# Latent attention's queries and keys as high and low parts, its logits in three fp32r passes in place of one fp32 product

## The chip, the cores and the metric

The kernel runs as one program on one NeuronCore of one Trainium2 chip. The metric is the device time of an execution in microseconds (us), the median of three runs. The profile is of one execution, taken by the hardware profiler; its times count from the start of the span. PE is the matrix engine (TensorE), ACT the ScalarE, DVE the VectorE, POOL the GpSimd, SP the engine that issues the loads.

## The reference

Two layers of a first kind (gated spatial mixing, a state-space mixer, differential attention, a feed-forward network) are followed by two layers of a second kind, over 512 positions and a width of 1024, in float32. The change lies in the second kind, in the logits of its latent attention:

```python
q = (rms_norm(q_lat, q_a_norm) @ w_qb).reshape(b, s, 8, 96)
kv = (rms_norm(kv_lat, kv_a_norm) @ w_kvb).reshape(b, s, 8, 64 + 64)
...
q, k = rms_norm(q, q_norm), rms_norm(k, k_norm)      # then rope on the last 32 of 96
sc = jnp.einsum('bqhd,bkhd->bhqk', qb, k) * 96 ** -0.5
sc = jnp.where(causal, sc, NEG_INF)
p = jax.nn.softmax(sc, axis=-1)
o = jnp.einsum('bhqk,bkhd->bqhd', p, v)
```

Beside it a layer has a short gated convolution and a sliding-window attention, each with a silu gate, and one output projection with a residual.

## The kernel before

Every large product is made of three passes of type fp32r: an operand x is kept as a high part (x rounded to fp32r) and a low part (x minus the high part), and `mm3` adds high x high, high x low and low x high in PSUM. Weights come by DMA in slabs of up to 1024 columns into a ring of four (`w_raw`); ACT writes the high part of a slab (`split_hi`, L564), DVE its low part over the raw one (`split_lo`, L569), three slabs ahead of PE (`hi_ahead`, `lo_ahead`).

The latent attention runs in sixteen steps of the loop `for g in range(FILLS)`, called fills here. Each engine has this loop in its own program, in a fixed order, and semaphores tie them together. Eight heads (h) times four blocks of 128 queries (qi) make 32 steps n = 4h + qi; fill g has steps 2g and 2g+1, so an even fill has the blocks with 128 and 256 keys of a head and an odd one those with 384 and 512. In a fill:

- PE multiplies one weight slab for the convolution or a gate (`slab_t`, eight groups k of three passes, L574 to L576). In an even fill it transposes, before group 5, the queries and the keys of head g/2 (`heads_t`, L674, four 128x96 transposes each) into two banks of PSUM. After the slab it waits until both banks have been read (`pm_left`), makes the logits of steps 2g and 2g+1 (L2439), and transposes the weights of the two steps before (`weights_t`, L674). Before group 6 of fills 5, 9 and 13 it multiplies the weights of two heads by V (`by_v`, L2413).
- ACT copies queries and keys of the head from PSUM to SBUF, times the norm's gain (`heads_in`, L1226), at the start of an even fill; copies transposed weights (`weights_in`, L1246) and takes the exponentials of the logits (`exponentials`, L1235); then splits a slab (`hi_ahead`).
- DVE takes the maximum of each row (`maximum`, L1865 to L1867), divides the exponentials by their sum (`weights`, L1873 and L1874), splits a slab (`lo_ahead`, L569), and does the convolution (L1842 to L1858) and the norm of the window attention (L1824 to L1833) in shares. `gated` (L1880), at the start of fills 5 and 9, multiplies the product with V by its gate and so frees its bank.

`qkt`, the queries and keys, has two buffers (h % 2). The four banks `pm` of PSUM are used in turn, in one fixed order for all engines: whoever wants the i-th use waits for the reader of use i - 4 (`take_pm`). So the banks of a head's transposes are those of the logits of the odd fill before, which the exponentials free; and the bank of a product with V is the one that the second transposes of weights in the same fill want.

Of the kernel before, what the change touches and what calls it, by code (L numbers as in the profile page):

```python
# [7 lines left out]
F32 = mybir.dt.float32  # L8
# [5 lines left out]
P = 128  # L14
# [99 lines left out]
def program(nc, t, out, depth=DEPTH, depth2=DEPTH):  # L114
    with ExitStack() as ctx:
# [62 lines left out]
        def at(off, n, shape=None, **kw):  # L178
            a = arena[:, off:off + n]
            return a.rearrange(shape, **kw) if shape else a  # L180
# [220 lines left out]
        sq2 = at(19456, 3072)  # L401
        mla_sq = [sq2, at(11264, 2048)]
        st2 = rinv[:, :]
        qkt = at(19456, 2048, "p (b c s) -> p b c s", b=2, c=2)

        PT_AT = [sum(SEQ - P * j for j in range(kt)) for kt in range(TT + 1)]
        pt = at(11264, 2 * PT_AT[TT], "p (b n) -> p b n", b=2)
# [84 lines left out]
        def gate_unit(i):  # L492
# [15 lines left out]
                "ffn_hi_done": KD, "ffn_split": KD, "f_tap": 2 * FT, "f_step": 4 * FT, "f_silu": FT, "f_val": FT, "f_hi_done": FT, "f_split": FT}  # L508
        PER2 = {"par_landed": 16 * 13, "h_val": KD, "h_hi_done": KD, "h_lo_dve": len(LO_DVE), "h_lo_pool": len(LO_POOL), "lat_rms": 1, "lat_ready": 2 * TT,
                "lat_hi_done": 3, "lat_split": 3, "k_rot": 6, "mla_sq": 2, "mla_ssq": 2, "mla_rms": 2, "mla_rot": 1, "swa_sq": 2, "swa_ssq": 2,  # L510
                "swa_rms": 1, "swa_kd": TT, "cv_free": 4, "neg_max": MLA_H * TT, "w_ready": MLA_H * TT, "y_hi_done": 12, "y_split": 12,
                "swa_gates": 2, "mla_gate": 1, "rope_tab": 8, "s_max": SWA_H, "s_exp": SWA_H, "s_w_ready": SWA_H * TT, "alibi_landed": 16}

        def steps_of(h):
# [26 lines left out]
        def pmb(i):  # L541
            return pm[:, i % 4, :]
# [118 lines left out]
        def pm_filled(eng, i):  # L661

            eng.wait_ge(pm_ready, i + 1)
            return pmb(i)
# [177 lines left out]
        def _(act):  # L842
            chain = Chain(act, "act_step")

            def hi_ahead(s, m=0, it=0):

                if s + LEAD < len(WORDS):
                    split_hi(act, s + LEAD, m, it, WORDS[s + LEAD + (m * it if isinstance(it, int) else 0)])
# [288 lines left out]
            for l in range(depth2):  # L1137
# [85 lines left out]
                def heads_in(h):  # L1223
                    for i in range(2):
                        u = PM2[("qk_t", h)] + i
                        nc.scalar.activation(qkt[0:MLA_QK, h % 2, i, :], pm_filled(act, u)[0:MLA_QK, :], ACT.Identity, scale=g_cols[0:MLA_QK, i:i + 1])\  # L1226
                            .then_inc(pm_free[u % 4], 1)

                def exponentials(n):

                    u, w, o = PM2[("score", n)], (n % TT + 1) * P, 128 + 4 * n
                    if n >= 3:
                        act.wait_ge(pm_ready, PM2[("w_t", n - 3)] + 1)
                    act.wait_ge(S("neg_max"), past("neg_max") + n + 1)
                    nc.scalar.activation(e2[n % 3][:, 0:w], pmb(u)[:, 0:w], ACT.Exp, bias=st2[:, o + 1:o + 2], scale=MLA_QK ** -0.5,  # L1235
                                         accum_out=st2[:, o + 2:o + 3]).then_inc(pm_free[u % 4], 1)

                def weights_in(n):
# [7 lines left out]
                        done = nc.scalar.activation(pt[:, h % 2, o:o + P], bank[:, kt * P:(kt + 1) * P], ACT.Copy)  # L1246
                    done.then_inc(pm_free[u % 4], 1)

                for g in range(FILLS):
                    if g % 2 == 0:  # L1250
                        heads_in(g // 2)
                    if g == FILLS - 1:
                        for i in range(6):
                            u = PM2["swa_t"] + i
                            if i < 4:
                                nc.scalar.activation(qts[:, i, :], pm_filled(act, u), ACT.Identity, scale=g_cols[:, 2:3]).then_inc(pm_free[u % 4], 1)
                            else:
                                nc.scalar.activation(kts[:, i - 4, :], pm_filled(act, u), ACT.Copy).then_inc(pm_free[u % 4], 1)
                    if g % 3 == 0 or g >= CONV_FILLS:
                        if 3 <= g < CONV_FILLS:  # L1260
                            unit_left(act, UN2["fill"] + g - 1)
                        dst = cv_h if g < CONV_FILLS else y2[:, 2, :] if g == CONV_FILLS else y2[:, 3 + g - CONV_FILLS, :]
                        nc.scalar.activation(dst, unit_filled(act, SL2["fill"] + g, UN2["fill"] + g), ACT.Copy).then_inc(bank_free[(UN2["fill"] + g) % BANKS], 1)
                    for n in (2 * g, 2 * g + 1):
                        if g >= 1:
                            weights_in(n - 2)
                        exponentials(n)
                    hi_ahead(SL2["fill"] + g)

                    if g == SWA_NORM:  # L1270
                        act.wait_ge(S("k_rot"), past("k_rot") + 6)
                        for sq_v, hs in zip(swa_sq, SWA_HEADS):
                            nc.scalar.activation(sq_v, swn[:, :, SWA_D * hs.start:SWA_D * hs.stop].rearrange("p t (h d) -> p t h d", d=SWA_D), ACT.Square)\
                                .then_inc(S("swa_sq"), 1)
                    if g == SWA_NORM + 2:
                        act.wait_ge(S("swa_ssq"), past("swa_ssq") + 2)
                        nc.scalar.activation(st2[:, 64:104], st2[:, 64:104], ACT.Sqrt, bias=eps[:, :], scale=1.0 / SWA_D).then_inc(S("swa_rms"), 1)
# [58 lines left out]
        def _(dve):  # L1336
# [404 lines left out]
            for l in range(depth2):  # L1741
# [140 lines left out]
                def y_high(i):  # L1882
                    nc.vector.tensor_copy(y2_hi[i], y2_val[i]).then_inc(S("y_hi_done"), 1)


                for g in range(FILLS):
                    if g in PV_AT[:2]:
                        gated(PV_AT.index(g))
                    if g == PV_AT[2]:
                        u = PM2[("pv", 2)]  # L1890
                        nc.vector.tensor_copy(pv_keep, pm_filled(dve, u)).then_inc(pm_free[u % 4], 1)
                    maximum(2 * g)
                    maximum(2 * g + 1)
                    weights(2 * g)
                    weights(2 * g + 1)
                    if g == FILLS - 1:
                        for j in range(MLA_H // 2 - 2):
                            pm_left(dve, PM2[("pv", j)])
                            y_high(j)
                    lo_ahead(SL2["fill"] + g)  # L1900
                    if g % 3 == 2 and g < CONV_FILLS:
                        conv_tile(g // 3, 0)
                    if g % 3 == 0 and 3 <= g <= CONV_FILLS:
                        conv_tile(g // 3 - 1, 1)
                    if g % 3 == 1 and 4 <= g <= CONV_FILLS + 1:
                        i = g // 3 - 1
                        conv_tile(i, 2)
                        dve.wait_ge(S("cv_free"), past("cv_free") + i + 1)
                        y_high(4 + i)
                    if g % 3 == 1 and g < CONV_FILLS:  # L1910
                        conv_gate(g // 3)
                    for part, late in enumerate((1, 3, 4, 5, 6, 7)):
                        if g == SWA_NORM + late:
                            swa_norm(part)
# [175 lines left out]
        def _(pe):  # L2090
# [275 lines left out]
            for l in range(depth2):  # L2366
# [51 lines left out]
                for g in range(FILLS):  # L2418
                    def between(k):
                        if k == 6 and g in PV_AT:  # L2420
                            by_v(PV_AT.index(g))
                        if k == 5 and g % 2 == 0:
                            if g == 0:
                                pe.wait_ge(S("mla_rot"), past("mla_rot") + 1)
                            heads_t(g // 2)
                        if g == FILLS - 1 and k >= 2:
                            i = k - 2
                            if i == 0:
                                pe.wait_ge(S("swa_kd"), past("swa_kd") + TT)
                            transposes(pe, PM2["swa_t"] + i, lambda bank: [(bank[:, tt * P:(tt + 1) * P], swn[:, tt, i * P:(i + 1) * P] if i < 4 else  # L2430
                                                                           kd[tt][:, (i - 4) * P:(i - 3) * P]) for tt in range(TT)])

                    slab_t(pe, SL2["fill"] + g, UN2["fill"] + g, 0, 0, hh, hl, KD, ready=between)
                    if g % 2 == 0:
                        pm_left(pe, PM2[("qk_t", g // 2)])
                        pm_left(pe, PM2[("qk_t", g // 2)] + 1)
                    for n in (2 * g, 2 * g + 1):
                        h, qi = n // TT, n % TT
                        nc.tensor.matmul(take_pm(pe, PM2[("score", n)])[:, 0:(qi + 1) * P], qkt[0:MLA_QK, h % 2, 0, qi * P:(qi + 1) * P],  # L2439
                                         qkt[0:MLA_QK, h % 2, 1, 0:(qi + 1) * P], start=True, stop=True).then_inc(pm_ready, 1)  # L2440
                    if g >= 1:
                        weights_t(2 * g - 2)
                        weights_t(2 * g - 1)
# [289 lines left out]
```

## Time and profile before

| | |
|---|---|
| runs | 2522.24, 2523.22, 2523.35 us, median 2523.22 |
| the profiled execution | 2523.0 us, span 2521.3 us |
| busy: PE, PE's weight loads | 2510.9 us (100%), 2056.3 us (82%) |
| busy: DVE, ACT, POOL | 1586.9 us (63%), 1185.3 us (47%), 317.7 us (13%) |
| granted clock of PE | 1.000 of full speed |
| fills of the two layers | about 1947 to 2077 us and 2281 to 2411 us |

In a timeline row stand the start, the duration, engine, line, operation, what is written from what, the shapes, and how many of them were merged; in brackets the idle time before and what ended it. PE's instructions overlap in the pipeline, so that their pitch (from start to start) and not their duration is what one of them costs; the pieces of the chain of waits show it directly. An fp32 matmul stands in the trace as two records, a transpose and an fp32r pass as one. Durations of DVE and ACT overlap by under 0.1 us in the same way.

### The profile page before, as it was taken

The numbers are of one execution on the slowest core, as the hardware profiler recorded it, in microseconds if no ns is written. First come the engines' busy times: TensorE is split into PE (matmuls) and PEld (weight loads), VectorE is DVE, ScalarE is ACT, GpSimd is POOL, SyncE is SP. The second block draws the span as 40 slices with busy tenths as digits, with TensorE's granted clock in tenths as the row PEclk, the third lists the DMA queues.
The fourth block names the chain that finished last, engine by engine and source line by source line (L and its number), as shares of the span: only waits on it lengthen the run. The fifth ranks groups of instructions, "written<-read, shape, count | busy, mean of one in ns | idle before, by whom it ended". The sixth has DMA issues, their size and how long they took to land.

```text
span 2521.3 us, 34195 instructions
## 1 busy us (share of the span) xinstructions
PE 2510.9 (100%) x12345; PEld 2056.3 (82%) x12345; DVE 1586.9 (63%) x2457; ACT 1185.3 (47%) x2187; POOL 317.7 (13%) x248
## 2 busy tenths in 40 slices
PE   9999999999999999999999999999999999999999
PEld 7887887888888887887877888888888777887777
DVE  6735767567777347537667567774345777647765
ACT  7534545544333235436354443333246555574563
POOL 1024201010111000225020101110010001210010
PEclk9999999999999999999999999999999999999999
DMA  6433342333333353452444433333324322333322
GB/s 143 97 81 68 85 91 76 67 110 92 100 92 98 99 109 89 87 79 72 90 81 69 95 92 100 92 100 96 97 80 105 85 67 61 87 96 76 84 59 76
DMA packets 400032, 221.96 MB, mean 88 GB/s; under 512 B 52736, under 2 KB 377376, under 8 KB 399648
## 3 DMA queue, kind: packets, MB, share of 16 engines
q1 hardware_dynamic: 399904, 220.26, 35.9%
q8 instruction: 80, 1.31, 0.2%
q14 instruction: 48, 0.39, 0.0%
HBM read 218.12 MB, written 2.10 MB: 87 GB/s over the span
## 4 chain that ended last, share of the span: by engine, by line
PE 96%; DVE 2%; DMA 1%; ACT 1%; issue 1%; SPq 0%; DVEq 0%; ACTq 0%
PE pg L574 28%; PE pg L576 28%; PE pg L575 28%; PE pm L674 3%; PE pm L2439 1%; PE pm L2323 1%; PE pm L2413 1%; PE pm L2235 1%; PE pm L2288 1%; DVE w_lo L569 1%; DMA w_raw<-in_w_in_dram 1%; PE pm L2453 1%; PE pm L2480 1%; PE pm L2238 0%; PE pm L2218 0%
## 5 line engine op out<-in xcount | busy, mean ns | idle before, releaser
L569 DVE TENSOR_TENSOR w_lo<-w_raw,w_hi 128x1024 fp32r<-128x1024 f32 (+3 forms) x440 | 540.4, 1229 | 519.8 <-ACT w_hi L564 517.5
L574 PE MATMUL pg<-h_hi,w_hi 128*128 128x512 f32 x1856 | 736.6, 397 | 0.3
L576 PE MATMUL pg<-h_hi,w_lo 128*128 128x512 f32 x1856 | 723.3, 390 | 0.0
L575 PE MATMUL pg<-h_lo,w_hi 128*128 128x512 f32 x1856 | 723.1, 390 | 0.0
L564 ACT ACTIVATE w_hi<-w_raw 128x1024 fp32r<-128x1024 f32 (+3 forms) x440 | 434.0, 988 | 588.9 <-DMA w_raw<-in_w_in_dram 247.2
L574 PEld LDWEIGHTS pg<-h_hi,w_hi 128*128 128x128 f32 x1856 | 348.6, 188 | 76.6 <-issue 8.4
L576 PEld LDWEIGHTS pg<-h_hi,w_lo 128*128 128x128 f32 x1856 | 348.4, 188 | 74.0
L575 PEld LDWEIGHTS pg<-h_lo,w_hi 128*128 128x128 f32 x1856 | 348.9, 188 | 68.8 <-issue 1.0
L574 PE MATMUL pg<-w_hi,h_hi 128*128 128x512 f32 (+2 forms) x440 | 164.1, 373 | 0.0
L575 PE MATMUL pg<-w_lo,h_hi 128*128 128x512 f32 (+2 forms) x440 | 162.0, 368 | 0.0
L576 PE MATMUL pg<-w_hi,h_lo 128*128 128x512 f32 (+2 forms) x440 | 161.9, 368 | 0.0
L1714 DVE SCALAR_TENSOR_TENSOR arena<-conv_in,par,arena 128x512 f32<-128x512 f32 x176 | 131.8, 749 | 15.2 <-DVE arena L1714 11.0
L574 PE MATMUL pg<-f_hi,w_hi 128*128 128x512 f32 x352 | 136.9, 389 | 0.0
L575 PE MATMUL pg<-f_lo,w_hi 128*128 128x512 f32 x352 | 136.9, 389 | 0.0
L576 PE MATMUL pg<-f_hi,w_lo 128*128 128x512 f32 x352 | 136.9, 389 | 0.0
L1120 ACT ACTIVATE arena<-conv_in,par 128x512 f32<-128x512 f32 x88 | 71.9, 817 | 124.1 <-DVE conv_in L1708 124.1
L558 POOL TENSOR_TENSOR f_lo<-arena,f_hi x44 | 56.9, 1293 | 518.1 <-DVE f_hi L1722 518.1
L1708 DVE TENSOR_TENSOR conv_in<-pg,rinv 128x512 f32<-128x512 f32 x88 | 60.8, 691 | 88.9 <-PE pg L576 79.8
L574 PE MATMUL pg<-nb_parts,w_hi 128*128 128x512 f32 x256 | 101.9, 398 | 0.0
L576 PE MATMUL pg<-nb_parts,w_lo 128*128 128x512 f32 x256 | 99.7, 389 | 0.0
L574 PEld LDWEIGHTS pg<-w_hi,h_hi 128*128 128x128 f32 x440 | 82.8, 188 | 12.9 <-issue 0.9
L576 PEld LDWEIGHTS pg<-w_hi,h_lo 128*128 128x128 f32 x440 | 82.8, 188 | 12.5
(410 smaller groups left out, 3748.4 us busy)
## 6 DMA issues: line engine op xcount, KB each, us to landing
w_raw<-in_w_in_dram SPq DMA_DIRECT2D x184, 512.0 KB, 4.7
w_raw<-in_ffn_w_up_dram SPq DMA_DIRECT2D x88, 512.0 KB, 3.7
w_raw<-in_w_out_dram SPq DMA_DIRECT2D x32, 512.0 KB, 3.8
w_raw<-in_ffn_w_down_dram SPq DMA_DIRECT2D x32, 512.0 KB, 3.9
w_raw<-in_w_branch_b_dram SPq DMA_DIRECT2D x16, 512.0 KB, 3.9
w_raw<-in_ffn_w_down_dram SPq DMA_DIRECT2D x16, 384.0 KB, 3.4
w_raw<-in_w_branch_a_dram SPq DMA_DIRECT2D x16, 256.0 KB, 2.8
w_raw<-in_w_branch_c_dram SPq DMA_DIRECT2D x16, 256.0 KB, 2.7
```

Source lines behind the costliest of these rows:

```text
L558: return nc.gpsimd.tensor_tensor(lo, value, hi.bitcast(F32), ALU.subtract)
L564: nc.scalar.activation(w_hi[:, s % HI, 0:n], w_raw[:, s % RAW, 0:n], ACT.Copy).then_inc(hi_done, 1)
L569: nc.vector.tensor_tensor(w_lo[:, s % RAW, 0:n], w_raw[:, s % RAW, 0:n], w_hi[:, s % HI, 0:n].bitcast(F32), ALU.subtract)\
L574: nc.tensor.matmul(dst, l_hi, r_hi, start=start, stop=False)
L575: nc.tensor.matmul(dst, l_hi, r_lo, start=False, stop=False)
L576: return nc.tensor.matmul(dst, l_lo, r_hi, start=False, stop=stop)
L674: done = nc.tensor.transpose(dst, src, ident[0:src.shape[0], 0:src.shape[0]])
L1120: nc.scalar.activation(facc[:, j, :], conv_in[:, j, 4:4 + SEQ], ACT.Identity, bias=fconv_b[:, bass.ds(i, 1)], scale=fconv_w[:, i, 2:3]).th ...
L1708: nc.vector.tensor_tensor(conv_in[:, j, 4:4 + SEQ], unit_filled(dve, SL["up"] + j, UN["up"] + j, 4, it), inv[:, :], ALU.mult)\
L1714: nc.vector.scalar_tensor_tensor(facc[:, j, :], conv_in[:, j, 4 - a:4 - a + SEQ], fconv_w[:, i, 2 - a:3 - a], facc[:, j, :], ALU.mult, ALU ...
L2235: done = nc.tensor.matmul(bank[rows, c * P:(c + 1) * P], xdt[:, c, h * 64:h * 64 + 64], seg[:, h % 4, c, :], start=True, stop=c == 0)
L2288: done = nc.tensor.matmul(bank[:, qi * P:(qi + 1) * P], wt(h, kt)[:, (qi - kt) * P:(qi - kt + 1) * P], qkv[:, kt, 1024 + h * P:1024 + (h + ...
```

## The change

`qkt` with its two buffers gives way to `qkt_hi` and `qkt_lo` in the same space, each with one buffer for queries and keys. ACT writes the high parts, rounded to fp32r, and no longer frees the bank; DVE has a new function, `head_lows`, that subtracts the high part from the bank times the gain, writes the low part and frees the bank. PE makes the logits with `mm3`. Since the single buffer is free only after the logits of the odd fill, `heads_in` and `head_lows` of the next head stand at the end of the odd fill, ahead of its `hi_ahead` and `lo_ahead`; those of head 0 stand ahead of the loop.

```diff
-        qkt = at(19456, 2048, "p (b c s) -> p b c s", b=2, c=2)
+        qkt_hi, qkt_lo = parts_at("qkt_hi", 19456, 2), parts_at("qkt_lo", 20480, 2)
...
                 def heads_in(h):
                     for i in range(2):
                         u = PM2[("qk_t", h)] + i
-                        nc.scalar.activation(qkt[0:MLA_QK, h % 2, i, :], pm_filled(act, u)[0:MLA_QK, :], ACT.Identity, scale=g_cols[0:MLA_QK, i:i + 1])\
-                            .then_inc(pm_free[u % 4], 1)
+                        nc.scalar.activation(qkt_hi[0:MLA_QK, i, :], pm_filled(act, u)[0:MLA_QK, :], ACT.Identity, scale=g_cols[0:MLA_QK, i:i + 1])\
+                            .then_inc(S("qkt_hi_done"), 1)
...
+                heads_in(0)
                 for g in range(FILLS):
-                    if g % 2 == 0:
-                        heads_in(g // 2)
...
                         exponentials(n)
+                    if g % 2 == 1 and g < FILLS - 1:
+                        heads_in(g // 2 + 1)
                     hi_ahead(SL2["fill"] + g)
...
+                def head_lows(h):
+
+                    for i in range(2):
+                        u = PM2[("qk_t", h)] + i
+                        dve.wait_ge(S("qkt_hi_done"), past("qkt_hi_done") + 2 * h + i + 1)
+                        nc.vector.scalar_tensor_tensor(qkt_lo[0:MLA_QK, i, :], pmb(u)[0:MLA_QK, :], g_cols[0:MLA_QK, i:i + 1],
+                                                       qkt_hi[0:MLA_QK, i, :].bitcast(F32), ALU.mult, ALU.subtract).then_inc(pm_free[u % 4], 1)
+
+                head_lows(0)
                 for g in range(FILLS):
...
+                    if g % 2 == 1 and g < FILLS - 1:
+                        head_lows(g // 2 + 1)
                     lo_ahead(SL2["fill"] + g)
...
-                        nc.tensor.matmul(take_pm(pe, PM2[("score", n)])[:, 0:(qi + 1) * P], qkt[0:MLA_QK, h % 2, 0, qi * P:(qi + 1) * P],
-                                         qkt[0:MLA_QK, h % 2, 1, 0:(qi + 1) * P], start=True, stop=True).then_inc(pm_ready, 1)
+                        q_hi, q_lo = (part[0:MLA_QK, 0, qi * P:(qi + 1) * P] for part in (qkt_hi, qkt_lo))
+                        k_hi, k_lo = (part[0:MLA_QK, 1, 0:(qi + 1) * P] for part in (qkt_hi, qkt_lo))
+                        mm3(take_pm(pe, PM2[("score", n)])[:, 0:(qi + 1) * P], q_hi, q_lo, k_hi, k_lo, True, True).then_inc(pm_ready, 1)
```

How the instructions move shows on DVE around the end of fill 7 of the first of the two layers. `L1873`/`L1874` (in the changed kernel `L1874`/`L1875`) are the weights of the fill's second step, `L569` the split of a slab, then come the convolution and the window norm, and `L1865` (`L1866`) begins the maxima of fill 8. Before:

```order
L1873 RECIPROCAL rinv<-rinv 128x1
L1874 TENSOR_SCALAR sq<-sq,rinv 128x512
L569 TENSOR_TENSOR w_lo<-w_raw,w_hi 128x1024
L1850 TENSOR_TENSOR arena<-arena,conv_in 128x512
L1883 CAST y_hi_cv<-arena 128x512
L1858 TENSOR_TENSOR arena<-arena,pg 128x512
L1831 TENSOR_TENSOR arena<-arena,rinv 128x640
L1833 TENSOR_TENSOR conv_in<-arena,par 128x256
L1865 TENSOR_TENSOR pm<-pm,c_pack 128x128
```

After, at the same place:

```order
L1874 RECIPROCAL rinv<-rinv 128x1
L1875 TENSOR_SCALAR sq<-sq,rinv 128x512
L1892 SCALAR_TENSOR_TENSOR qkt_lo<-pm,consts,qkt_hi 96x512 x2
L569 TENSOR_TENSOR w_lo<-w_raw,w_hi 128x1024
L1851 TENSOR_TENSOR arena<-arena,conv_in 128x512
L1884 CAST y_hi_cv<-arena 128x512
L1859 TENSOR_TENSOR arena<-arena,pg 128x512
L1832 TENSOR_TENSOR arena<-arena,rinv 128x640
L1834 TENSOR_TENSOR conv_in<-arena,par 128x256
L1866 TENSOR_TENSOR pm<-pm,c_pack 128x128
```

The two low parts of head 4 stand ahead of the split and all that follows, and nothing else has changed places. On ACT, at the end of an odd fill (`L1235` the second exponential, `L564` the split of a slab, `L1226` the copies of queries and keys), before:

```order
L1246 ACTIVATE arena<-pm 128x128 x2
L1235 ACTIVATE sq,rinv<-pm,rinv 128x512
L564 ACTIVATE w_hi<-w_raw 128x1024
L1226 ACTIVATE arena<-pm,consts 96x512 x2
L1246 ACTIVATE arena<-pm 128x128 x3
```

and after:

```order
L1246 ACTIVATE arena<-pm 128x128 x2
L1235 ACTIVATE sq,rinv<-pm,rinv 128x512
L1226 ACTIVATE qkt_hi<-pm,consts 96x512 x2
L564 ACTIVATE w_hi<-w_raw 128x1024
L1246 ACTIVATE arena<-pm 128x128 x3
```

The copies and the split have changed places. On PE the order is kept, and in place of the two fp32 products of an even fill (its last slab group ahead of them) stand six passes; after:

```order
L576 MATMUL pg<-h_hi,w_lo 128x512
L574 MATMUL pm<-qkt_hi 128x128
L575 MATMUL pm<-qkt_lo,qkt_hi 128x128
L576 MATMUL pm<-qkt_hi,qkt_lo 128x128
L574 MATMUL pm<-qkt_hi 128x256
L575 MATMUL pm<-qkt_lo,qkt_hi 128x256
L576 MATMUL pm<-qkt_hi,qkt_lo 128x256
```

Each of the six brings its own weights, the 128 columns of a block of queries.

## Rows read from the trace of the kernel before

**Rows 1.** The page: busy time of the engines, and the chain that ended last.
```profile
PE 2510.9 (100%) x12345; PEld 2056.3 (82%) x12345; DVE 1586.9 (63%) x2457; ACT 1185.3 (47%) x2187; POOL 317.7 (13%) x248
...
PE 96%; DVE 2%; DMA 1%; ACT 1%; issue 1%; SPq 0%; DVEq 0%; ACTq 0%
```

**Rows 2.** The chain of waits (start, length, what, count): logits, even and odd fill.
```profile
1953.23 0.66 PE pm L2439 x4
...
1959.35 1.51 PE pm L2439 x4
```

**Rows 3.** The chain: fp32r passes of 512, of 256 columns, fp32 records of 32.
```profile
1951.18 0.23 PE pg L574
...
1898.76 0.12 PE pg L574
...
574.23 0.81 PE pm L747 x8
```

**Rows 4.** Timeline: a head handed over, and high and low parts made elsewhere.
```profile
1950.14 1.04 PE L674 MATMUL pm<-c_pack,arena 128*96 128x128 f32 x8
...
1953.07 0.82 PE L2439 MATMUL pm<-arena 96*128 96x128 f32 x4
...
1950.78 1.26 ACT L1226 ACTIVATE arena<-pm,consts 96x512 f32<-96x512 f32 x2 [2.29 <-PE pm L674]
...
1410.95 0.69 ACT L1084 ACTIVATE nb_parts<-pm,par 128x512 fp32r<-128x512 f32 x1 [0.45 <-PE pm L674]
...
1411.04 1.40 DVE L1663 SCALAR_TENSOR_TENSOR yc_lo<-pm,par,nb_parts 128x512 fp32r<-128x512 f32 x2
```

**Rows 5.** Timeline of DVE in fills 4 to 11, and an exponential's end on ACT.
```profile
1988.27 0.68 DVE L1850 TENSOR_TENSOR arena<-arena,conv_in 128x512 f32<-128x512 f32 x1
...
1989.93 2.87 DVE L1824 TENSOR_REDUCE rinv<-arena 128x32 f32<-128x2048 f32 x2
1992.72 0.68 DVE L1880 TENSOR_TENSOR arena<-arena,pm 128x512 f32<-128x512 f32 x1
...
2014.56 0.68 DVE L1850 TENSOR_TENSOR arena<-arena,conv_in 128x512 f32<-128x512 f32 x1
...
2018.12 0.29 DVE L1865 TENSOR_TENSOR pm<-pm,c_pack 128x128 f32<-128x128 f32 x1
...
2021.58 1.23 DVE L569 TENSOR_TENSOR w_lo<-w_raw,w_hi 128x1024 fp32r<-128x1024 f32 x1 [0.40 <-ACT w_hi L564]
2022.72 0.68 DVE L1842 TENSOR_TENSOR conv_in<-pg,conv_in 128x512 f32<-128x512 f32 x1
...
2025.87 0.30 DVE L1865 TENSOR_TENSOR pm<-pm,c_pack 128x128 f32<-128x128 f32 x1
...
2031.06 1.53 DVE L1847 SCALAR_TENSOR_TENSOR conv_in<-conv_in,par 128x512 f32<-128x512 f32 x2
...
2033.84 0.29 DVE L1865 TENSOR_TENSOR pm<-pm,c_pack 128x128 f32<-128x128 f32 x1
...
2042.23 0.29 DVE L1865 TENSOR_TENSOR pm<-pm,c_pack 128x128 f32<-128x128 f32 x1
...
2045.11 0.19 ACT L1235 ACTIVATION_READ_ACCUMULATOR rms<-pm,rinv 128x1 f32 x1
```

**Rows 6.** Timeline of PE: transposes of heads 2, 4, 5, 6 and of steps 9, 17.
```profile
1979.56 0.81 PE L674 MATMUL pm<-c_pack,arena 128*96 128x128 f32 x6
...
1993.90 0.38 PE L674 MATMUL pm<-c_pack,sq 128*128 128x128 f32 x2
...
2012.65 1.03 PE L674 MATMUL pm<-c_pack,arena 128*96 128x128 f32 x8
...
2026.64 0.38 PE L674 MATMUL pm<-c_pack,rms 128*128 128x128 f32 x2
...
2030.29 0.81 PE L674 MATMUL pm<-c_pack,arena 128*96 128x128 f32 x6
...
2045.39 1.03 PE L674 MATMUL pm<-c_pack,arena 128*96 128x128 f32 x8
```

More of the change, by code:

```diff
@@ L510, in program @@
                 "lat_hi_done": 3, "lat_split": 3, "k_rot": 6, "mla_sq": 2, "mla_ssq": 2, "mla_rms": 2, "mla_rot": 1, "swa_sq": 2, "swa_ssq": 2,
-                "swa_rms": 1, "swa_kd": TT, "cv_free": 4, "neg_max": MLA_H * TT, "w_ready": MLA_H * TT, "y_hi_done": 12, "y_split": 12,
+                "swa_rms": 1, "swa_kd": TT, "qkt_hi_done": 2 * MLA_H, "cv_free": 4, "neg_max": MLA_H * TT, "w_ready": MLA_H * TT, "y_hi_done": 12, "y_split": 12,
                 "swa_gates": 2, "mla_gate": 1, "rope_tab": 8, "s_max": SWA_H, "s_exp": SWA_H, "s_w_ready": SWA_H * TT, "alibi_landed": 16}
```

## The prediction

> **What bounds the kernel now.** I read the page first: TensorE (PE) is busy for all of the span, and the chain of work that ended last lies on it for 96% [rows 1]. So whatever the change takes off PE's queue counts in full, as long as PE stays the engine that is waited for. The page's shares hide the exception. In the timeline of the latent attention (sixteen "fills" for each of two layers, a fill being one slab of weights on PE with the logits of two steps behind it) the VectorE (DVE) is the second engine. In fills 7 to 12 it goes from one piece of work to the next with hardly a gap, and its maxima start long after the logits are there. So I read three things: what a pass costs [rows 2, 3], how a head gets from PE over ScalarE (ACT) and back [rows 4], and DVE's turn through fills 7 to 12 [rows 5] beside the places where PE needs something of it [rows 6].
>
> **The passes.** Before, the logits of an even fill (128 and 256 columns) take 0.66 us, those of an odd fill (384 and 512) 1.51 us [rows 2]: 0.22, 0.44, 0.65 and 0.86 us for the four widths. After, each is three fp32r passes. One of 512 columns takes 0.23 us, one of 256 takes 0.12 [rows 3], and 384 lies between them at 0.175. Odd fill: 3 x 0.175 + 3 x 0.23 = 1.21 us, 0.30 less. No fp32r pass of 128 columns is in the trace. From below it is bounded by the line through 256 and 512 (0.11 us for 256 columns, so 0.055 for 128 fewer): 0.065. From above by what fp32 pays for 128 columns: 0.22. The nearest row is that of 32 columns, eight records with a load of 128 columns of weights before each, in 0.81 us [rows 3]: 0.10 to 0.11 for each though the columns would stream in much less, so the load sets it. I take 0.11. Even fill: 3 x 0.11 + 3 x 0.12 = 0.69, 0.03 more. A head (two fills) gains 0.27 us, and 16 heads 4.3 us. With 0.065 they gain 6.5 us, with 0.22 they lose 1.0.
> On that width two rules of the Trainium skill disagree (page "TensorE: Matmul & The Clock Gate"). The section "LDWEIGHTS (loading the stationary operand)" gives a load by its columns, 107 ns for 128, and the trace's 32-column row agrees. The section "Back-to-back issue gap" gives a sustained 81 ns for 128 columns. By it an even fill would take 0.60 us, and the passes of all heads together 1.4 us less than I count; no row here shows it for this type.
>
> **The hand-over of a head.** T is the start of the transposes of queries and keys. ACT starts on the queries at T+0.64 and has both copied at T+1.90 [rows 4]. Before, that was all that PE waited for at T+2.93 (1953.07 against 1950.14), its slab being done. After, DVE subtracts each high part from the same PSUM bank. The trace has this very operation elsewhere: high part by ACT, low part by DVE from PSUM, 0.74 us, starting 0.06 us after ACT's end, and two in a row take 1.40 [rows 4]. So the second low part ends at T+1.90+0.06+0.74 = T+2.70, or T+2.8 behind the first. With 0.1 us until PE takes it up this just fits into 2.93. Price: nothing where both engines are idle (bounds 0 and 0.1 us a head, 0 and 1.6 in all).
>
> **What queues behind it.** This is where I see the cost. DVE runs in order, and the low parts of the next head now stand in each odd fill between its last weights and its split of a weight slab (L569). They wait for PE's transposes of the next slab, so everything behind them waits as well: the split, the convolution and window norm of that fill, and only then the maxima of the even fill. Before, DVE did all that while PE reached the transposes. PE waits for DVE in turn at two places. It cannot transpose the next head before the exponentials of the odd fill have freed the two PSUM banks (four banks in turn), and those wait for the maxima; and after a product with V its bank must be freed by `gated` before the weights of an odd step can be transposed.
> DVE's turn, from rows 5. Low parts: DVE's split starts when ACT's is done, which now stands behind the two copies: T+1.81+1.05, plus 0.04, and takes 1.14 (2022.72 - 2021.58), so DVE is through at T+4.05. From the first maximum of an even fill to the end of its split: 2018.12 to 2022.72, 4.60. From the first maximum of an odd fill to the end of its second exponential: 2042.23 to 2045.30, 3.07. Between these lies the fill's own work: 3.56 in fills 7 and 10 (2014.56 to 2018.12), 3.15 in fill 8 (2022.72 to 2025.87), 2.78 in fill 9 (2031.06 to 2033.84), and by the same kinds of operation about 1.2 in fill 5 and 2.0 in fill 6. Now one layer, d being how late PE is against before:
> - Heads 0 and 1 gain 0.27 each: d = -0.54 at T of head 2.
> - Fills 3 to 5: 4.05 + 1.57 (two steps of the convolution, as in fill 9) + 4.60 + 1.66 (three operations, from 1988.27) + 2.79 (the sums of squares, from 1989.93) + 0.68 (`gated`) + 0.11 = 15.46 until PE has the bank for step 9. Before, it took it 14.34 after T (1993.90 - 1979.56) [rows 6]. d = -0.54 + 15.46 - 14.34 = +0.58.
> - Fills 5 to 7 hold less: 4.05 + 1.2 + 4.60 + 2.0 + 3.07 = 14.9 against PE's own 15.10 - 0.27 (two fills without a product with V: 2045.39 - 2030.29). No wait; d = +0.31 at 2012.65.
> - Fills 7 to 9: 4.05 + 3.56 + 4.60 + 3.15 + 0.11 = 15.47. PE has the bank for step 17 at 2012.96 + 15.47 = 2028.43; before it took it at 2026.64. d = +1.79.
> - Fills 9 to 12: 2032.08 + 4.05 + 2.78 + 4.60 + 3.56 + 3.07 = 2050.14 for the exponentials that free the banks of head 6. ACT then starts on the keys 0.74 us later (0.1 for PE to begin, 0.44 of transposes, 0.2 until ACT sees them) and not at T+1.22, so T counts as 0.48 earlier, 2049.66, and d = +4.27, from 2045.39. This is the largest wait, 2.7 us.
> - Fills 12 to 15: DVE has little of its own there and a product with V gives it 2.3 us. PE gains 0.27 and 0.30 again, but its first transposes of the window attention need the bank of the first exponential of fill 14, and DVE comes to that one at T + 4.05 + 1.06 (three operations less 0.6) + 1.2, some 0.6 too late. d = +4.3.
> Two layers: +8.6 us. The profiled execution took 2523.0 us (span 2521.3 and 1.7 around it), the median is 2523.2. The sum gives 2531.6 for the one and 2531.8 for the other. The two layers have one shape before, so I count them alike. The numbers go by an uninterrupted PE; I cost the smaller buffers, the longer lifetime of `pm` banks in the hand-over and the 64 more matmuls beyond that at nothing, since PE waits for both banks anyway.
> As PE is no longer the bound in fills 3 to 12, the price of the narrow pass hardly matters: 0.22 would change only the heads where PE is ahead, by about 0.3 us each, +2 in all. The other uncertain terms are the 0.1 us of each hand-over and how ACT's table loads (1.28 us) fall, together 1 to 3 us each way. Own range: 2528 to 2537.
>
> **Rivals.**
> A, the queues absorb it: DVE's delay is made good in the gaps, and PE never waits. Then the passes count: -4.3, 2518.9, with a cheap narrow pass 2516.7. For it: DVE is busy for only 63% of the span [rows 1]. Against it: in fills 7 to 10 the maxima follow on the work before them without a gap [rows 5]. It decides from the point where DVE's own work in two fills stays under some 3.5 us; that holds for fills 5 and 6 only. Chance 0.10.
> B, a part only: the waits are half as long, because DVE's and ACT's operations overlap more closely than I add them. The three waits of a layer come to 1.4 + 1.7 + 2.7 = 5.8 us (the differences of d with PE's gains between them); half of them in both layers are 5.8 us less: 2526. Chance 0.12.
> C, the narrow pass runs at fp32's price and the queues absorb the rest: 16 x 0.06 lost, 2524. Nothing speaks for it but that the trace has no such pass. Chance 0.08.
> D, the change does not do what it says, in that three passes cost as much as fp32 at every width, because each brings its own load of weights. It would show as odd fills near 1.5 us and, DVE setting the pace of fills 3 to 12, add some 0.3 us for each of the eight other heads: 2534, inside the forecast's range.
>
> **How the numbers follow.** Forecast 0.70, A 0.10, B 0.12, C 0.08. Measurements of this kernel tell a change from none at about 0.2%, 5 us: below 2518.2 counts as faster, above 2528.3 as slower. A's time lies just beside the first bound and gives a good half of its chance to faster; B and C give theirs mostly to the same. Forecast, nearly all of it, to slower. Faster 0.08, same 0.20, slower 0.72. The range from 2521 to 2537 leaves out A and a little above.
>
> **What would show it.** Logits of an even fill at 0.7 us and of an odd one at 1.2. ACT's idle time at L1226 larger than before. DVE's maxima of even fills starting 2 to 5 us after the logits. PE, which hardly idles before, waiting about 1.4 us before the transposes of step 9, 1.7 in all before those of step 17 (part of it before the second product with V), and 2.7 before those of head 6, and in both layers alike. Wrong is the whole chain of reasons if PE has no idle time in these fills, whatever the time is; wrong in its size only, if the waits are there and differ.

## The result and the profile after

The changed kernel takes 2536.48 us (median of five runs, 2535.78 to 2538.04), the kernel before 2522.35 in the same session: a ratio of 1.0057, with a 95% interval from 1.0042 to 1.0072. It is 14 us slower; the forecast's sum was 2531.8, with a range from 2521 to 2537. The profiled execution has a span of 2534.7 us, 13.4 more than before.

The page of the changed kernel, in answer to [rows 1]: busy time, and the chain that ended last.

```profile
PE 2511.6 (99%) x12409; PEld 2065.0 (81%) x12409; DVE 1608.2 (63%) x2489; ACT 1187.8 (47%) x2187; POOL 316.0 (12%) x248
...
PE 91%; DVE 5%; ACT 2%; issue 1%; DMA 0%; SPq 0%; ACTq 0%; DVEq 0%
```

PE works as long as before and the span is longer: the chain now runs over DVE and ACT for 7% of it (3% before). The list of PE's waits of the changed kernel (who waits, for whom: us in total, times, longest) says where:

```profile
PE pm L674 <- ACT sq L1235: 6.1, 6, 1.8
PE pm L674 <- DVE arena L1881: 4.0, 4, 1.6
...
PE pm L2425 <- ACT arena L1246: 1.9, 2, 0.9
PE pm L674 <- ACT rms L1235: 1.2, 2, 0.6
```

None of these four was among the waits before, and together they are 13.2 us. They come in both layers at the same places. The timeline of PE in the first layer, in answer to [rows 6] (the idle time and what ended it in brackets; L674 are transposes, L2425 is the product with V):

```profile
1993.01 0.41 PE L674 MATMUL pm<-c_pack,sq 128*128 128x128 f32 x2 [1.57 <-DVE arena L1881]
...
2012.98 0.65 PE L674 MATMUL pm<-c_pack,arena 128*96 128x128 f32 x4 [0.58 <-ACT sq L1235]
...
2022.23 2.38 PE L2425 MATMUL pm<-arena 128*64 128x512 f32 x16 [0.93 <-ACT arena L1246]
...
2027.93 0.41 PE L674 MATMUL pm<-c_pack,rms 128*128 128x128 f32 x2 [0.41 <-DVE arena L1881]
...
2048.50 0.64 PE L674 MATMUL pm<-c_pack,arena 128*96 128x128 f32 x4 [1.84 <-ACT sq L1235]
2049.73 1.09 PE L674 MATMUL pm<-c_pack,arena 128*96 128x128 f32 x4 [0.58 <-ACT rms L1235]
2050.47 0.78 PE L574 MATMUL pg<-h_hi,w_hi 128*128 128x512 f32 x1
2051.04 0.63 PE L575 MATMUL pg<-h_lo,w_hi 128*128 128x512 f32 x1
...
2053.80 0.22 PE L574 MATMUL pm<-qkt_hi 96*128 96x128 f32 x1
...
2074.84 0.63 PE L674 MATMUL pm<-c_pack,arena 128*128 128x128 f32 x4 [0.62 <-ACT sq L1235]
```

The first is step 9 waiting for `gated`, 1.57 where 1.4 was forecast. At 2012.98 the keys of head 4 wait, which was not forecast. The third and fourth belong to step 17, 1.34 together where 1.7 was forecast. At 2048.50 and 2049.73 queries and keys of head 6 wait, 2.42 in all where 2.7 was forecast. The row at 2051.04 has the other surprise: passes whose pitch is 0.23 us elsewhere have one of 0.42 to 0.57 for over 2 us.

The table sets PE's lateness d against the kernel before at T, the start of a head's transposes, relative to head 0 of the same layer. (At head 0 of the first layer this execution of the changed kernel was 1.54 us ahead. That lies before the fills and differs between executions: in the eleven traces of this case head 0 starts at 1948.6 to 1950.1.) The last column goes from head 0 to head 0 of the next layer, or to the end.

| d at head | 1 | 2 | 3 | 4 | 5 | 6 | 7 | whole layer |
|---|---|---|---|---|---|---|---|---|
| forecast | -0.27 | -0.54 | +0.58 | +0.31 | +1.79 | +4.27 | | +4.3 |
| after, first layer | -0.23 | -0.49 | +0.69 | +0.65 | +2.89 | +4.66 | +6.77 | +7.7 |
| after, second layer | -0.25 | -0.48 | +0.70 | +0.66 | +2.89 | +4.66 | +6.62 | +7.3 |

### The profile page after: what moved, and what is told of

Its sections match the earlier page's. It is cut to its first block, busy times and chain, and to the rows that moved or that the text cites. A ratio compares the mean times of both kernels' runs of the same rounds, so it can differ in the third digit from the quotient of the medians.

```text
span 2534.7 us, 34355 instructions
## 1 busy us (share of the span) xinstructions
PE 2511.6 (99%) x12409; PEld 2065.0 (81%) x12409; DVE 1608.2 (63%) x2489; ACT 1187.8 (47%) x2187; POOL 316.0 (12%) x248
## 3 DMA queue, kind: packets, MB, share of 16 engines
q8 instruction: 80, 1.31, 0.2%
## 4 chain that ended last, share of the span: by engine, by line
PE 91%; DVE 5%; ACT 2%; issue 1%; DMA 0%; SPq 0%; ACTq 0%; DVEq 0%
PE pg L574 27%; PE pg L576 27%; PE pg L575 27%; PE pm L674 3%; DVE w_lo L569 1%; ACT w_hi L564 1%; PE pm L2335 1%; PE pm L2300 1%; PE pm L2247 1%; PE pm L2466 1%; PE pm L2493 1%; PE pm L2250 0%; PE pm L2230 0%; PE pm L2222 0%; PE pm L2425 0%
## 5 line engine op out<-in xcount | busy, mean ns | idle before, releaser
L569 DVE TENSOR_TENSOR w_lo<-w_raw,w_hi 128x1024 fp32r<-128x1024 f32 (+3 forms) x440 | 540.7, 1230 | 515.2 <-ACT w_hi L564 512.0
L564 ACT ACTIVATE w_hi<-w_raw 128x1024 fp32r<-128x1024 f32 (+3 forms) x440 | 433.8, 987 | 588.3 <-DMA w_raw<-in_w_in_dram 245.9
```

Of the source, the lines that this page charges most:

```text
L564: nc.scalar.activation(w_hi[:, s % HI, 0:n], w_raw[:, s % RAW, 0:n], ACT.Copy).then_inc(hi_done, 1)
L569: nc.vector.tensor_tensor(w_lo[:, s % RAW, 0:n], w_raw[:, s % RAW, 0:n], w_hi[:, s % HI, 0:n].bitcast(F32), ALU.subtract)\
```

## The experiments

Times are medians; each ratio is to the kernel before on the same chip. Three edits of the change are told apart: the order (ACT's copies of a head ahead of its split of a slab), DVE's low parts, and the passes.

**e1: the move alone.** The kernel before with a single buffer and the copies moved as in the change, but fp32 logits and no low parts.

```diff
+                heads_in(0)
                 for g in range(FILLS):
-                    if g % 2 == 0:
-                        heads_in(g // 2)
...
+                    if g % 2 == 1 and g < FILLS - 1:
+                        heads_in(g // 2 + 1)
                     hi_ahead(SL2["fill"] + g)
...
-   ... qkt[0:MLA_QK, h % 2, 0, ...], qkt[0:MLA_QK, h % 2, 1, ...]
+   ... qkt[0:MLA_QK, 0, 0, ...], qkt[0:MLA_QK, 0, 1, ...]
```

> The kernel before (fp32 logits, no low parts, DVE's work and order untouched) with one buffer for queries and keys and ACT's copies of the next head moved to the end of the odd fill, ahead of its slab split. Theory O (the delay comes from the order: ACT's split of the slab now stands behind copies that wait for PE, and DVE's split and all that follows waits for it): as slow as the changed kernel or slower, since the gain of the passes is missing: +14 to +18 us, with the same waits of PE (steps 9 and 17, heads 4 and 6). Rival L (the delay comes from the low parts, DVE's own 1.4 us per head): within 1 us of the kernel before.

Measured: 2537.77 us, ratio 1.0057 (1.0043 to 1.0071). A loss of 15 us is there without a single low part. PE waits at the same places but one: 1.32 us at step 9, 0.57 at the keys of head 4, 1.00 before the second product with V, 1.59 and 0.58 at head 6, 0.68 in fill 15; the 0.41 of step 17 is missing. The largest line of its list of PE's waits, beside 6.1, 6, 1.8 in the changed kernel:

```profile
PE pm L674 <- ACT sq L1235: 5.7, 6, 1.6
```

Timeline of DVE in e1 at the end of fill 7 (second weights, then the split of a slab):

```profile
2014.97 0.49 DVE L1875 TENSOR_SCALAR sq<-sq,rinv 128x512 f32<-128x512 f32 x1
2017.14 1.23 DVE L569 TENSOR_TENSOR w_lo<-w_raw,w_hi 128x1024 fp32r<-128x1024 f32 x1 [1.68 <-ACT w_hi L564]
```

and the same two, with the low parts between, in the changed kernel:

```profile
2013.16 0.49 DVE L1875 TENSOR_SCALAR sq<-sq,rinv 128x512 f32<-128x512 f32 x1
2013.57 1.57 DVE L1892 SCALAR_TENSOR_TENSOR qkt_lo<-pm,consts,qkt_hi 96x512 fp32r<-96x512 f32 x2
2015.34 1.23 DVE L569 TENSOR_TENSOR w_lo<-w_raw,w_hi 128x1024 fp32r<-128x1024 f32 x1 [0.20 <-ACT w_hi L564]
```

From the second weights to the split it is 2.17 us in the one and 2.18 in the other. DVE waits for ACT's half of the split, which now stands behind copies that wait for PE. The low parts merely fill a wait that the order has made.

**e2: the window norm spread out.** The changed kernel with the six shares of DVE's window norm in even fills, to relieve fills 7 to 12.

```diff
-                    for part, late in enumerate((1, 3, 4, 5, 6, 7)):
+                    for part, late in enumerate((1, 3, 5, 7, 9, 11)):
```

> The changed kernel with the shares of the window norm in fills 4, 6, 8, 10, 12, 14 in place of 4, 6, 7, 8, 9, 10; nothing else. Theory (DVE's turn through fills 7 to 12 is what PE waits for): the wait before head 6 shrinks from 2.0 + 0.75 us to under 1 us, the wait before the second product with V goes, the wait for step 9 stays; PE's clock stays full; 3 us less a layer by the queues and 1.2 by the clock, 2528 us. Rival (the handing over of each head costs, not the work between): no change, 2536.

Measured: 2543.37 us, ratio 1.0083 (1.0069 to 1.0097), a miss of 15 us. The wait for head 6 did shrink (1.05 us from the start of the last pass to that of the transposes, where it was 2.22), and the one before the second product with V went, but the list of PE's waits of e2 begins with a new one:

```profile
PE pm L674 <- DVE arena L1834: 10.1, 2, 5.1
```

The last share, in fill 14, is ready too late for the window attention's transposes in fill 15. Five us in each layer are lost there, and PE's clock is down behind it (granted clock 0.50 from 2073 to 2079).

**e3: the splits first.** The changed kernel, in which each odd fill has the split of the slab ahead of the head, on both engines.

```diff
 (ACT)
+                    hi_ahead(SL2["fill"] + g)
                     if g % 2 == 1 and g < FILLS - 1:
                         heads_in(g // 2 + 1)
-                    hi_ahead(SL2["fill"] + g)
 (DVE)
+                    lo_ahead(SL2["fill"] + g)
                     if g % 2 == 1 and g < FILLS - 1:
                         head_lows(g // 2 + 1)
-                    lo_ahead(SL2["fill"] + g)
```

> The changed kernel with the splits of the odd fill's slab ahead of the copies on ACT and ahead of the low parts on DVE. Theory O: the delay shrinks though DVE does the same work: 3.4 us less a layer and 1.2 of clock, 2527 us; what is left waits at head 6, and 0.2 to 1.1 us at the logits of heads 4 to 6, where the low parts come late. Rival L: no change, 2536, since the low parts are still made.

Measured: 2527.3 us (11 runs), ratio 1.0018 (1.0009 to 1.0028). On each of the two engines two pieces change places, and that takes 9.2 us off. Some 3 of them are PE's clock, which falls once a layer in the trace of the changed kernel, at about 1.5 us each (last section); e3 has it at 1.000 in all eleven executions. The other 6 or so are waits. Timeline of DVE in e3 at the end of fill 7:

```profile
2012.12 1.23 DVE L569 TENSOR_TENSOR w_lo<-w_raw,w_hi 128x1024 fp32r<-128x1024 f32 x1 [0.26 <-ACT w_hi L564]
2013.26 1.40 DVE L1892 SCALAR_TENSOR_TENSOR qkt_lo<-pm,consts,qkt_hi 96x512 fp32r<-96x512 f32 x2
```

The split runs at once. The low parts of head 4 are now late by themselves, so that PE waits for them with its first logits (and 0.87 us with those of head 6, whose transposes still wait 0.51 and 0.59):

```profile
2014.77 0.30 PE L574 MATMUL pm<-qkt_hi 96*128 96x128 f32 x1 [0.61 <-issue]
```

**e4: both.** e3 with e2's shares.

```diff
 (the two of e3)
-                    for part, late in enumerate((1, 3, 4, 5, 6, 7)):
+                    for part, late in enumerate((1, 3, 5, 7, 9, 11)):
```

> Both: splits first and the window norm spread over the even fills. Theory O: PE waits for under 1.5 us a layer and the passes' gain of 2.1 us a layer shows for the most part: 2520 to 2522 us, at or just below the kernel before. Rival L: like the spread alone, 2528.

Measured: 2535.95 us, ratio 1.0052 (1.0039 to 1.0066), a miss, for e2's reason (line of PE's waits in e4):

```profile
PE pm L674 <- DVE arena L1834: 7.6, 2, 3.8
```

**e5: the last shares in fills 11 and 12.** e3 with shares in fills 4, 6, 7, 8, 11 and 12: fills 9 and 10 are relieved, and the last share keeps its distance from fill 15.

```diff
 (the two of e3)
-                    for part, late in enumerate((1, 3, 4, 5, 6, 7)):
+                    for part, late in enumerate((1, 3, 4, 5, 8, 9)):
```

> The changed kernel with the splits first, and with the window norm's last two shares in fills 11 and 12 in place of 9 and 10 (shares in fills 4, 6, 7, 8, 11, 12), so that they are done well before the window attention's transposes in fill 15. Theory (DVE's turn through fills 9 to 12 makes the wait at head 6, the late end of the norm made the one in fill 15): no wait of over 1 us is left at head 6 or in fill 15, PE's clock stays full, 2 us less a layer than with the splits alone (2527.3): 2521 to 2524 us. Rival (the shares cannot be moved without the wait turning up elsewhere): 2527 or more.

Measured: 2522.39 us (11 runs), ratio 1.0000 (0.9991 to 1.0009), as expected. The loss of the change is gone, and its arithmetic is kept. One PE wait in the fills is still over half a us, in each layer, for the low parts of head 4 (timeline of PE in e5):

```profile
2014.03 0.30 PE L574 MATMUL pm<-qkt_hi 96*128 96x128 f32 x1 [0.61 <-issue]
```

**e6: the passes alone.** The kernel before, order and two buffers kept, with logits of three passes. It leaves out the low parts: all three passes read the high ones.

```diff
-   nc.tensor.matmul(take_pm(...), qkt[..., h % 2, 0, ...], qkt[..., h % 2, 1, ...], start=True, stop=True)
+   q_hi, k_hi = qkt[h % 2][0:MLA_QK, 0, ...], qkt[h % 2][0:MLA_QK, 1, ...]
+   mm3(take_pm(...), q_hi, q_hi, k_hi, k_hi, True, True)
```

> The kernel before in order and buffers, with the logits in three fp32r passes that all take the high parts (the low parts are left out). Only PE's passes change. Theory: 0.69 us in place of 0.66 for an even fill, 1.21 in place of 1.51 for an odd one, 4.3 us less in all, and the 0.3 us before head 2 stays: 2518 us. Rival (an fp32r pass of 128 columns runs at fp32's price, or the gain is hidden by DVE): 2522 to 2524 us.

Measured: 2520.32 us (11 runs), ratio 0.9992 (0.9983 to 1.0001), 2.4 us where 4.3 were counted. Six of the seven steps from head to head gain 0.17 to 0.27 us, as counted; the one to head 3 gains 0.02. Between the layers 0.8 us is given back: timeline of ACT and of PE in e6 at the start of the second layer:

```profile
2229.95 1.06 ACT L564 ACTIVATE w_hi<-w_raw 128x1024 fp32r<-128x1024 f32 x1 [2.92 <-DMA w_raw<-in_mla_w_qb_dram]
2230.92 1.19 ACT L1168 ACTIVATE arena<-pg 128x256 f32<-128x256 f32 x4
...
2231.43 0.47 PE L574 MATMUL pg<-h_hi,w_hi 128*128 128x512 f32 x1 [0.54 <-ACT arena L1168]
```

ACT's split waits for a slab from the DMA, ACT's copies stand behind it, and PE, which comes earlier now, waits for those.

**e7: splits first, no low parts.** e3 with the low parts of head 0 read for all heads; those of heads 1 to 7 are left out.

```diff
-                            .then_inc(S("qkt_hi_done"), 1)
+                            .then_inc(pm_free[u % 4] if h else S("qkt_hi_done"), 1)
...
-                    if g % 2 == 1 and g < FILLS - 1:
-                        head_lows(g // 2 + 1)
```

> The changed kernel with the splits first and without DVE's low parts from the second head on (ACT's copy frees the bank; the low parts of the first head are used for all). Theory O: what the low parts cost by themselves is the difference to the run with the splits first and the low parts (2527.3), some 3.5 us a layer by the queues: 2519 us, no wait of PE over 0.3 us. Rival (with the splits first the low parts are free, and what is left there is the single buffer): 2526 us.

Measured: 2518.42 us (11 runs), ratio 0.9985 (0.9976 to 0.9994). That is 8.9 less than e3: with the splits first, the low parts cost that much, and without them the change would be a small gain. e7 keeps the single buffer, and no wait of PE over 0.2 us is left in its fills; so the buffer by itself costs nothing. The two costs don't add. Against e7, which has neither, the low parts alone cost 8.9 us (e3) and both together some 18 (the changed kernel); the order alone costs 15 against the kernel before (e1, with fp32 logits), and 15 and 8.9 would be 24. In the changed kernel the low parts hide in the wait that e1 shows.

**e8: a table load out of the way.** What the forecast missed in fill 6 stands in the timeline of DVE of the changed kernel (end of the split of fill 5; first maximum; first reciprocal; split; first maximum of fill 7):

```profile
1999.58 1.22 DVE L569 TENSOR_TENSOR w_lo<-w_raw,w_hi 128x1024 fp32r<-128x1024 f32 x1
...
2001.96 0.30 DVE L1866 TENSOR_TENSOR pm<-pm,c_pack 128x128 f32<-128x128 f32 x1
...
2004.64 0.16 DVE L1874 RECIPROCAL rinv<-rinv 128x1 f32<-128x1 f32 x1 [1.01 <-ACT sq L1235]
...
2006.71 1.23 DVE L569 TENSOR_TENSOR w_lo<-w_raw,w_hi 128x1024 fp32r<-128x1024 f32 x1 [0.40 <-ACT w_hi L564]
...
2009.86 0.30 DVE L1866 TENSOR_TENSOR pm<-pm,c_pack 128x128 f32<-128x128 f32 x1
```

and in that of ACT:

```profile
2002.85 1.28 ACT L1235 ACT_TABLE_LOAD   x1 [0.31 <-DVE rinv L1868]
2004.14 0.37 ACT L1235 ACTIVATE sq<-pm,rinv 128x128 f32<-128x128 f32 x1
```

The window norm's square root in fill 5 has put another table in, so the exponentials of fill 6 start with a load, and DVE waits behind it. The timeline of ACT before has it too:

```profile
2002.36 1.28 ACT L1235 ACT_TABLE_LOAD   x1
```

There DVE was ahead and had the time. e8 is the changed kernel with the square root at the end of fill 6, followed by a one-column exponential into an unused column that has the table loaded again while nobody waits.

```diff
-                    if g == SWA_NORM + 2:
+                    if g == SWA_NORM + 3:
                         act.wait_ge(S("swa_ssq"), past("swa_ssq") + 2)
                         nc.scalar.activation(st2[:, 64:104], st2[:, 64:104], ACT.Sqrt, ...).then_inc(S("swa_rms"), 1)
+                        nc.scalar.activation(st2[:, 500 + l:501 + l], eps[:, :], ACT.Exp)
```

> The changed kernel with one thing moved: the square root of the window norm (ACT, L1278) stands at the end of fill 6 in place of fill 5, and a one-column exponential into an unused column follows it, so that the table is loaded again while ACT has nothing to do. The trace of the changed kernel has the load for the exponentials of fill 6 at 2002.85 to 2004.13 in front of them, and DVE idle for 1.01 us behind it; DVE's even fill 6 (first maximum to the end of its split) took 5.98 us there (2001.96 to 2007.94) against the 4.60 that the prediction counted. Theory: that 1.38 is what the prediction's sum lacks in the wait of head 4's keys (0.58) and, through the next fills, in the lateness of head 5 and of head 6. Then fill 6 takes DVE 4.6, the keys of head 4 follow the queries at once, PE's wait for head 6 is shorter by about 1.1, and if the fall of the clock behind it depends on that wait, it goes as well. 2536.5 less 2 x 1.1 = 2534.3 with the fall of the clock, less 2 x 1.5 more = 2531.3 without it. Rival: the table load only fills time in which the exponentials would wait for something else, and the time stays at 2536.5 within 1.

Measured: 2537.07 us (2533.82 to 2538.52), ratio 1.0058 (1.0044 to 1.0072). In the timeline of DVE in e8, fill 6 takes from 2002.83 to 2007.53, 4.70:

```profile
2002.83 0.30 DVE L1867 TENSOR_TENSOR pm<-pm,c_pack 128x128 f32<-128x128 f32 x1
...
2006.30 1.23 DVE L569 TENSOR_TENSOR w_lo<-w_raw,w_hi 128x1024 fp32r<-128x1024 f32 x1 [0.40 <-ACT w_hi L564]
```

The keys of head 4 don't wait, and d at heads 4 to 7 is +0.49, +2.01, +3.76, +4.40 in the first layer and within 0.1 of that in the second: 0.9 less than the changed kernel at heads 5 and 6, and 2.3 to 2.4 less at head 7, since the clock didn't fall. Against the expectation, PE's idle time at the queries of head 6 stayed at 1.83; the 0.9 was won before it. The traced execution is the shortest of the five (2533.82), and the median shows no gain. The granted clock of each execution was measured as well: 1.000 in the traced one, 0.998, 0.999, 0.998 and 0.998 in the other four, where the changed kernel has 0.999 in four and 1.000 in one. So the clock did fall in those at 0.998, no less than in the changed kernel, whose trace with two falls has 0.9986. At 1.5 us a fall that is enough to hide a gain of 1.8 in the median; where in these executions it fell is not shown. The two executions at 1.000 are 2535.78 us for the changed kernel and 2533.82 for e8, 2.0 apart, near the 1.8 that the trace shows, but they are single ones. The theory holds for the trace, the expected time is a miss.

**e9: e5 with the same move.**

```diff
 (e5, and the edit of e8)
```

> The version with the splits first and the norm's last shares in fills 11 and 12, with the square root moved to the end of fill 6 in the same way. In its profile the one wait of the fills near 1 us is that of head 4's first logits for the low parts (pitch 1.00, so 0.77 idle, in each layer), behind the same late fill 6. If the table load is its cause, it goes in both layers: 2522.4 less 1.5 = 2520.9, below the kernel before by 0.06%. Rival: the wait of head 4 has its cause in fill 7 alone, and the time stays at 2522.4.

Measured: 2521.8 us (11 runs), ratio 0.9996 (0.9987 to 1.0005). The wait at head 4 is gone in both layers, as expected (timeline of PE in e9):

```profile
2013.78 0.39 PE L576 MATMUL pg<-h_hi,w_lo 128*128 128x512 f32 x1
2014.01 0.22 PE L574 MATMUL pm<-qkt_hi 96*128 96x128 f32 x1
```

In the traces d at head 7 is -1.15 against -0.27 in e5, the 0.8 us a layer that was expected; the median is 0.6 us below e5's where 1.5 was expected, and not to be told from the kernel before. No version here that keeps the low parts beats the kernel before by a measurable amount.

## Why the prediction was right, and where its sum was off

**Passes: right.** Timeline of PE in the changed kernel, the logits of fills 0 and 1 and what comes behind, in answer to [rows 2, 3]:

```profile
1951.55 0.23 PE L574 MATMUL pm<-qkt_hi 96*128 96x128 f32 x1
1951.61 0.27 PE L575 MATMUL pm<-qkt_lo,qkt_hi 96*128 96x128 f32 x1
1951.72 0.27 PE L576 MATMUL pm<-qkt_hi,qkt_lo 96*128 96x128 f32 x1
1951.83 0.34 PE L574 MATMUL pm<-qkt_hi 96*128 96x256 f32 x1
...
1952.24 0.40 PE L574 MATMUL pg<-h_hi,w_hi 128*128 128x512 f32 x1
...
1957.70 0.34 PE L574 MATMUL pm<-qkt_hi 96*128 96x384 f32 x1
...
1958.92 0.49 PE L674 MATMUL pm<-c_pack,sq 128*128 128x128 f32 x3
```

0.69 us (1952.24 - 1951.55) and 1.22, forecast 0.69 and 1.21. A pass of 128 columns has a pitch of 0.11. Of the two rules of the Trainium skill that the prediction weighed (page "TensorE: Matmul & The Clock Gate"), that of "LDWEIGHTS (loading the stationary operand)", 107 ns, agrees with the 0.11 us, and the sustained 81 ns of "Back-to-back issue gap" does not.

**Hand-over: right.** Head 3 has T = 1996.70, and its low parts end at 1999.46, T+2.76, forecast 2.70 to 2.8. The first logits of head 0 start 2.95 after its T (1951.55 - 1948.60), against 2.93 before [rows 4]. It costs nothing, as counted.

**DVE's turn: right in its parts, one term too small.** For the stretch from T of head 3 to the exponentials that free the banks of head 4, the prediction added 4.05 + 1.2 + 4.60 + 2.0 + 3.07 = 14.9 and found no wait. The rows shown with e8 give 4.10 (the split ends at 2000.80), 1.16, 5.98 (2001.96 to 2007.94) and 1.92, and 3.07 follow: 16.2. All terms but one are within 0.1. The 4.60 of fill 6 came from another even fill [rows 5]; this one has the table load in it. The prediction named the table loads only as an uncertainty. Head 4's queries wait for it by 0.2 us (they start 0.42 behind the last pass, which is 0.23 elsewhere) and its keys by 0.58; d(T4) is +0.65 instead of +0.31 and d(T5) +2.89 instead of +1.79. e8 takes the load away, and 0.9 of the 1.1 goes.

**Step 9: right** (d at head 3 is +0.7, forecast +0.58). **Head 6: right in its place.** d(T6) of +4.27 was reckoned from when the keys can be handed over; by that measure it is about +5.4 (the keys start 1.23 behind the queries, some 0.8 more than before). The excess of 1.1 is the one carried over from head 5.

**The clock: missing.** From the keys of head 6 to the first logits behind them it takes 4.07 us in the changed kernel (2053.80 - 2049.73) and 2.55 in e8, where the clock stayed up. These 1.5 us a layer were in no term. The window attention's transposes wait 0.62, forecast 0.6.

So a layer costs 7.3 to 7.7, not 4.3: 1.1 from the table load, 1.5 from the clock, and 0.4 to 0.8 in small parts. Less the 1.5 us by which this execution was ahead at the first head, the sum of 14.9 is the 13.4 of the spans. The step of the prediction that was off is the sum of fills 5 to 7 ("No wait; d = +0.31"), and with it the price at head 5; the fall of the clock behind the largest wait was not thought of. The three waits that were forecast came at their places and near their sizes; that the time still lies in the range, by half a us, is in part luck, since 3 of the 14 us come from the clock, which no term had.

**The cause: right in the chain, less so in its weight.** The prediction set out from the low parts and had ACT's split behind the two copies as a mere term ("T+1.81+1.05"). e1 shows that this term is enough by itself: nearly the same waits and the same time come without low parts. e3 shows that the order is worth 9.2 us, clock included, and e7 that the low parts cost 8.9 once it is mended.

**Rivals.** A (the queues absorb it) is ruled out by the waits. B (waits half as long) as well: the three waits named are 1.57, 1.34 and 2.42. C and D fall with the passes, at 0.69 and 1.22. Both layers are alike, as assumed.

## What to carry to other kernels

On an in-order engine, an instruction that waits for another engine belongs behind the work that is ready: moving the ready split ahead of the waiting copies on ACT, and ahead of the waiting low parts on DVE, was worth 9 us of a loss of 14, more than the 4.3 counted for the passes. A duration taken from a like stretch must be looked up in the stretch itself; the table load stood in the trace of before at that very place, harmless there because DVE had time. Work that is put off in time to relieve one consumer has a last consumer of its own (e2 and e4), whose distance must be counted first.

## What the hardware showed that was not expected

**PE's clock fell behind some waits and not behind others like them.** Windows of the changed kernel (stretch, length, busy time and count of PE, PEld, DVE, ACT, POOL, then the granted clock, DMA share, GB/s), the stretch of the wait at head 6, the one behind it, and the next:

```profile
2048.00:2050.40 2.40, 1.31 (x8) 1.03 (x8) 1.92 (x7) 2.13 (x7) 0.00 (x0) 0.83 0.00 0
2050.40:2053.80 3.40, 3.40 (x11) 2.75 (x10) 2.68 (x4) 1.63 (x2) 0.00 (x0) 0.62 0.00 0
2054.00:2059.00 5.00, 5.00 (x30) 4.36 (x29) 3.86 (x13) 3.75 (x13) 0.00 (x0) 1.00 0.41 105
```

The windows of e8 at the same place, behind idle times of 1.83 and 0.59 us (1.84 and 0.58 in the changed kernel):

```profile
2048.00:2050.40 2.40, 1.33 (x9) 1.07 (x10) 1.92 (x7) 2.12 (x8) 0.00 (x0) 1.00 0.00 0
2050.40:2053.80 3.40, 3.40 (x23) 3.04 (x22) 3.12 (x4) 2.48 (x5) 0.00 (x0) 1.00 0.09 9
```

and of e1, behind 1.59 and 0.58 in the first layer and 1.59 and 0.59 in the second:

```profile
2050.00:2056.00 6.00, 5.11 (x31) 4.30 (x32) 3.81 (x9) 4.78 (x13) 0.00 (x0) 1.00 0.09 11
...
2391.00:2397.00 6.00, 5.41 (x22) 4.31 (x23) 3.52 (x9) 3.69 (x8) 0.00 (x0) 0.72 0.00 0
```

While it is down, the granted clock is 0.50 of full speed (1.2 instead of 2.4 GHz) and passes of 512 columns have a pitch of 0.43 instead of 0.23. A fall costs about 1.5 us: 4.07 less 2.55 above, and in e1 1.6, the second layer's way from head 6 to head 7 less the first's. In e2 it fell behind its two waits of 5 us and in the second layer behind the 1.56 of step 9, though not behind the same 1.56 in the first; in e4 it fell behind its two of 3.8. It stayed up in both layers behind the 1.57 of step 9 in the changed kernel. So waits of 1.6 to 1.8 us had a fall behind them in some places and none in others; what decides it, no run here shows. It adds a part to a wait's price that differs between executions.

**A table load took 1.28 us, with no gap beside it.** Timeline of ACT in e8, where a load and its function stand behind a split:

```profile
2005.17 1.10 ACT L564 ACTIVATE w_hi<-w_raw 128x1024 fp32r<-128x1024 f32 x1
2006.28 1.28 ACT L1278 ACT_TABLE_LOAD   x1
2007.58 0.33 ACT L1278 ACTIVATE rinv<-rinv,consts 128x40 f32<-128x40 f32 x1
```

From the end of the split to the start of the square root it is 1.31 us. The Trainium skill (page "ScalarE: Activation LUTs", section "What ACT_TABLE_LOAD costs") gives about 1283 ns for the load, with which the row agrees, and about 1380 ns for a drain beside it, of which these rows show nothing.
